# A hybrid diffusion layer on one core: a triangular inversion spread over all four quarters of the matmul array, and narrow products issued as two column halves

## The chip, the core and the metric

The kernel runs on one core of one Trainium2 chip. The metric is the device time of one launch in microseconds, lower is better. A core has a matmul engine (PE in the rows, with its weight loads as PEld), a vector engine (DVE), a scalar engine (ACT), a general engine (POOL), and a queue for transfers (SP). Each runs its own instruction stream in order; they wait for one another through semaphores.

## What is computed

One layer of a hybrid backbone for 512 latent tokens and 128 context tokens. It modulates and projects the tokens, sends them through three mixers (a bidirectional RWKV-7 recurrence, neighbourhood attention, a state-space model), gates and merges them, normalises, and applies a mixture of experts. The part that matters here is the recurrence, per head and per direction:

```python
def step(s, inp):
    r_t, w_t, k_t, v_t, kk_t, b_t = inp
    sa = jnp.einsum('bhvk,bhk->bhv', s, kk_t)
    s = s * w_t[:, :, None, :] - sa[..., None] * b_t[:, :, None, :] + v_t[..., None] * k_t[:, :, None, :]
    return s, jnp.einsum('bhvk,bhk->bhv', s, r_t)
```

The kernel does it in chunks of 128 tokens. Within a chunk the term `sa` makes a 128x128 triangular system per head, and its inverse is built by products of small blocks. The attention is an ordinary softmax over 512 local and 128 context keys per block of 128 queries, then a weighted sum of values of width 64.

## The kernel before

The launch is a row of phases with barriers between them: projections and preparations, the state-space scan, `rwkv_phase`, merge and router, experts, combine. The change lies in `rwkv_phase` alone, in the functions `rwkv_units` and `attention_lane`. Everything is float32; a product (`matmul`) leaves two records on PE in the trace and two weight loads on PEld.

`rwkv_units` walks through ten units (`UNITS`): five chunks of 128 tokens, each in two directions. A unit holds eight heads, as four pairs `q` with two heads `e` each; the head dimension of 64 makes `e` the lower or the upper 64 partitions (`half`). On PE a unit is, in this order:

- five Gram groups `k` = 0 to 4 at L1725, eight products each (64 rows, 128 stationary, 128 moving columns), into the four PSUM banks `bank[0..3]`; k = 0 and 1 are the system matrix and its transpose, and ACT (L1975, L1977), DVE (L1887) and POOL (L2062, L2064) make from them the blocks `lo`, `lc`, `xi`, `yi`;
- two groups of transposes (L1732), four narrow products for a bonus term (L1737, 2 moving columns);
- the inversion of the two 64x64 diagonal blocks in five levels (`LJ - 1`). A level is the group G (L1755, 16 products of 64x64x64 for the eight heads), ACT's copy of it (L1991), then for g = 0 and 1 the groups YG (L1786) and XG (L1791), eight products each; DVE subtracts them from `yi` (L1918) and `xi` (L1920). POOL makes the next level's masked block `lj` (L2071). A product's row half is where its operands lie, its column half is where its output lies; before, both are the same half in all three groups;
- the coupling block of the inverse (L1752 and a last L1786), which uses one quarter of the array;
- the right-hand sides and outputs: L1764 and L1798 (64 rows, 128 stationary, 64 moving), L1767, L1801 and L1819 (128 rows, 128 stationary, 64 moving), eight products each, and the solves and states L1806, L1809, L1814, L1824.

Between these groups PE issues fillers, and each other engine does its share of them at the same points of its own stream. A gate filler ("G", L1349 and L1350) is a piece of a sigmoid gate's product, eight turns for a tile, of which the eighth is empty on PE; ACT applies the sigmoid there. An attention filler ("A") is one of three steps in turn: scores (L1502, L1505), then the weighted sum of the previous block (L1476, L1477, L1479), then the transposes of the probabilities (L1515, L1518). DVE (L1555, L1556, L1558) and ACT (L1597) do the softmax between scores and transposes. Every level has "GA" between G and YG (`FILL_MID`) and "A" after XG (`FILL_LEVEL`). Of 40 attention blocks every fifth is for context queries and has only 128 keys.

## Time and profile before

| | us |
|---|---|
| median of three runs | 2099.69 |
| lowest and highest run | 2098.58, 2108.48 |
| the profiled run, its own time | 2100.16 |
| its span | 2096.8 |
| the ten units, 591.1 to 1219.3 in the span | 628.2 |

The page gives busy times for each engine and the span. The units were located in the timeline of PE by the first Gram products. A timeline row has the start, the duration from the first start to the last end, the engine, line, names, shape and count of records. Matmuls are pipelined, so the last end lies some 0.2 us behind the last issue; the time that a group takes from PE is read from its start to the start of the next group. The granted clock of a stretch is 1.00 at 2.4 GHz and 0.50 at 1.2 GHz.

### The profile page before, as it was taken

What the parts mean: (1) busy time and instruction counts of PE and PEld (TensorE: products, weight loads), DVE (VectorE), ACT (ScalarE), POOL (GpSimd) and SP (SyncE); (2) the same over time, 40 slices, a digit from 0 to 9 for tenths busy, and PEclk for the clock granted to TensorE, in tenths of its full rate; (3) what the DMA queues carried; (4) which work ended last, traced back from release to release, by engine and by line L of the source; (5) the groups of instructions that cost most, each with busy time, mean ns of one, the idle gap of its engine ahead of it and who ended that gap; (6) DMA issues with size and microseconds to landing.
All of it is one profiled execution on the core that took longest, in us unless ns stands there. A gap on an engine that the chain in (4) does not pass through costs nothing. (4 is left out here: it accounts for less than half of the span.)

```text
span 2096.8 us, 40476 instructions
## 1 busy us (share of the span) xinstructions
PE 1914.2 (91%) x15900; PEld 1408.1 (67%) x15900; DVE 1019.3 (49%) x2092; ACT 495.4 (24%) x936; POOL 690.8 (33%) x1036
## 2 busy tenths in 40 slices
PE   7999999888889999999999958998699999999966
PEld 2555655464668877888888738855578888878732
DVE  3868676648345435544555443645622222222238
ACT  2111132130223333433343321101112122112100
POOL 4526000000034323343333223322244454444435
PEclk9999999999899999999999979998799999999988
DMA  9143647473142210222120029610399989999855
GB/s 289 55 136 120 214 160 270 139 271 98 41 139 65 85 48 23 72 69 72 49 74 8 22 95 318 214 43 21 139 358 339 331 303 316 338 339 321 321 227 242
DMA packets 228303, 355.64 MB, mean 170 GB/s; under 512 B 38305, under 2 KB 156852, under 8 KB 224452
## 3 DMA queue, kind: packets, MB, share of 16 engines
q1 hardware_dynamic: 201358, 300.73, 42.2%
q0 software_dynamic: 24496, 45.01, 6.1%
q10 hardware_dynamic: 2310, 7.92, 1.0%
q8 instruction: 102, 1.67, 0.3%
q14 instruction: 37, 0.30, 0.0%
HBM read 307.11 MB, written 84.34 MB: 187 GB/s over the span
## 5 line engine op out<-in xcount | busy, mean ns | idle before, releaser
L2850 DVE TENSOR_TENSOR me_hh<-me_sg,ps_ju 128x128 f32<-128x128 f32 x76 | 21.9, 288 | 386.1 <-PE ps_jd L2802 374.3
L452 PE MATMUL ps_s<-hT,w_in_sb 128*128 128x512 f32 x432 | 194.7, 604 | 0.0
L2794 PE MATMUL ps_jg<-me_xT,me_wg 128*128 128x128 f32 x1216 | 149.3, 276 | 0.0
L1349 PE MATMUL ps_gs<-hT,gt_w 128*128 128x512 f32 x256 | 146.0, 653 | 3.2 <-PEq L76 3.2
L2794 PE MATMUL ps_ju<-me_xT,me_wu 128*128 128x128 f32 x1216 | 148.2, 275 | 0.0
L2802 PE MATMUL ps_jd<-me_wd,me_hh 128*128 128x512 f32 x304 | 143.1, 593 | 2.4 <-DVE me_yb L2856 2.4
L452 PEld LDWEIGHTS ps_s<-hT,w_in_sb 128*128 128x128 f32 x432 | 81.6, 194 | 93.5 <-issue 92.9
L2794 PEld LDWEIGHTS ps_jg<-me_xT,me_wg 128*128 128x128 f32 x1216 | 143.0, 193 | 0.0
L2794 PEld LDWEIGHTS ps_ju<-me_xT,me_wu 128*128 128x128 f32 x1216 | 141.9, 192 | 0.0
L2823 ACT ACTIVATE me_xT<-ps_jx 128x1024 f32<-128x1024 f32 x77 | 78.9, 1025 | 210.4 <-PE ps_jx L2785 210.4
L2785 PEld LDWEIGHTS ps_jx<-ident,me_xg 128*128 128x128 f32 x616 | 79.3, 191 | 69.8 <-DMA me_xg<-h_dram,me_ids 40.6
L2742 POOL TENSOR_TENSOR me_scr<-me_scr 128x1 f32<-128x1 f32 x312 | 61.0, 195 | 185.0 <-DVE me_yb L2856 168.4
L2071 POOL TENSOR_TENSOR rc_lj<-rc_l,rc_lev 128x256 f32<-128x256 f32 x100 | 75.1, 770 | 135.9 <-PE ps_c L1755 135.7
L2785 PE MATMUL ps_jx<-ident,me_xg 128*128 128x128 f32 x616 | 84.7, 281 | 26.6 <-DMA me_xg<-h_dram,me_ids 26.4
L922 DVE SCALAR_TENSOR_TENSOR ad_part<-w_ad_sb,c_silu,ad_part 128x256 f32<-128x256 f32 x224 | 105.2, 511 | 5.8 <-DMA w_ad_sb<-in_w_ada 2.3
L1154 POOL DMA_DIRECT2D out_new_s_re<-s_zz x1 | 0.6, 579 | 312.7 <-DVE s_zz L1218 312.7
L2750 POOL DMA_INDIRECT me_xg<-h_dram,me_ids x80 | 84.3, 1053 | 39.9 <-issue 36.9
L2856 DVE COPY me_yb<-ps_jd 128x1024 f32<-128x1024 f32 x76 | 92.8, 1221 | 4.2 <-issue 4.2
L1350 PEld LDWEIGHTS ps_gp<-hT,gt_w 128*128 128x128 f32 x256 | 50.4, 197 | 64.8 <-issue 64.8
L2761 POOL DMA_INDIRECT yj_dram<-me_yb,me_outs x76 | 77.5, 1020 | 43.4 <-issue 43.4
L2802 PEld LDWEIGHTS ps_jd<-me_wd,me_hh 128*128 128x128 f32 x304 | 52.0, 191 | 39.6 <-issue 36.3
L2030 POOL TENSOR_TENSOR rc_a<-ru_kk,rc_ex 128x512 f32<-128x512 f32 x10 | 12.6, 1265 | 196.8 <-ACT rc_fs L1963 196.8
(569 smaller groups left out, 3985.8 us busy)
## 6 DMA issues: line engine op xcount, KB each, us to landing
me_wg<-in_exp_w_gate SPq DMA_DIRECT2D x76, 512.0 KB, 5.6
me_wu<-in_exp_w_up SPq DMA_DIRECT2D x76, 512.0 KB, 7.7
me_wd<-in_exp_w_down SPq DMA_DIRECT2D x76, 512.0 KB, 6.0
w_ad_sb<-in_w_ada SPq DMA_DIRECT2D x32, 512.0 KB, 4.0
w_in_sb<-in_w_in SPq DMA_DIRECT2D x31, 512.0 KB, 4.4
gt_w<-in_w_in SPq DMA_DIRECT2D x24, 512.0 KB, 4.5
cb_rows<-yj_dram SPq DMA_DIRECT2D x6, 2048.0 KB, 22.0
zr<-in_w_ada SPq DMA_DIRECT2D x4, 2048.0 KB, 8.9
```

The lines of the kernel that those rows point to most:

```text
L452: mm(ps_s[:, b, :], w_in[:, r, k, :], hT[:, k, 0:TS], start=(k == 0), stop=(k == KT - 1))
L922: last = V.scalar_tensor_tensor(o, x, r, o, ALU.mult, ALU.add)
L1349: nc.tensor.matmul(ps_s[:], w[:, t % WR, k, :], hT[:, k, 0:TS], start=(k == 0), stop=(k == KT - 1))
L2071: G.tensor_tensor(lj[:, g], lo[:, g], bc4(levc[:, d, j + 1]), ALU.mult).then_inc(m.c_lj, 1)
L2742: G.tensor_tensor(scr[:, c:c + 1], scr[:, 2:3], scr[:, 2:3], ALU.add)
L2750: G.indirect_dma_start(xg[:, s], None, m.h2_dram, bass.IndirectOffsetOnAxis(ids[:, s:s + 1], axis=0), bounds_check=N - 1, oob_is_err=False ...
L2761: G.indirect_dma_start(m.yj_dram, bass.IndirectOffsetOnAxis(outs[:, b:b + 1], axis=0), yb[:, b], None, bounds_check=N * TOPK - 1, oob_is_e ...
L2785: last = nc.tensor.transpose(ps_x[:, s % 2, k * P:(k + 1) * P], xg[:, s, k:D:KT], m.ident[:])
L2794: last = mm(o[:, 0:P], w[:, s, k, :], xT[:, s % 2, k, :], start=(k == 0), stop=(k == KT - 1))
L2802: last = mm(ps_d[:, ts512(h)], hh[:], wd[:, s, ts512(h)], start=True, stop=True)
L2823: nc.scalar.activation(xT[:, s], ps_x[:, s].rearrange("p (k c) -> p k c", k=KT), ACT.Identity).then_inc(m.j_xt, 1)
L2856: V.tensor_copy(yb[:, b], ps_d[:]).then_inc(m.j_y, 1)
```

## The change

Four things change, all inside the units and the attention filler.

1. G's products write into the other column half than their row half. YG's products go from one row half to the other column half, XG's stay in theirs, and YG and XG are issued in turns, four products for each `q`, so that the four of a turn lie in four different quarters.
2. The Gram groups k = 0 and 1 are cut into 64x64x64 products: 32 for k = 0 (the diagonal blocks twice, once for `lo` in their own partitions and once for `xi` in the other half's) and 24 for k = 1. ACT copies `lo` and `xi` whole and then `lc`, for which it waits for DVE's product on `yi`; DVE makes `yi` in one instruction instead of two; POOL scales `xi` in place.
3. `halves` issues a product with 128 stationary columns as two with 64 each, into the lower and the upper 64 output partitions. It is used for L1737, L1764, L1767, L1798, L1801, L1819 and the attention's weighted sum.
4. DVE subtracts both `yi` first and then both `xi`, where before it went y, x, y, x.

```diff
+def halves(mm, out, l, r, start, stop):
+
+    for b in (slice(0, HD), slice(HD, P)):
+        last = mm(out[b], l[:, b], r, start=start, stop=stop)
+    return last
...
         o = ps_y[:, P:P + HD]
         if i < QT:
             for k in range(4):
-                nc.tensor.matmul(o, pT[:, k * P:(k + 1) * P], zv[:, b, k, hc], start=(k == 0), stop=False)
-            nc.tensor.matmul(o, pT[:, TS:TS + P], cv_sb[:, h, :], start=False, stop=True).then_inc(m.n_pv, 1)
+                halves(nc.tensor.matmul, o, pT[:, k * P:(k + 1) * P], zv[:, b, k, hc], k == 0, False)
+            halves(nc.tensor.matmul, o, pT[:, TS:TS + P], cv_sb[:, h, :], False, True).then_inc(m.n_pv, 1)
         else:
-            nc.tensor.matmul(o, pT[:, TS:TS + P], zv[:, b, QT, hc], start=True, stop=True).then_inc(m.n_pv, 1)
+            halves(nc.tensor.matmul, o, pT[:, TS:TS + P], zv[:, b, QT, hc], True, True).then_inc(m.n_pv, 1)
...
-                    for k, (l, r) in enumerate(((a_, b_), (b_, a_), (k_, a_), (k_, r_), (b_, r_))):
...
+                    rows, cols = coupling(d)
+                    if n:
+                        pe.wait_ge(m.c_un, n)
+                        pe.wait_ge(m.c_s, n)
+                    for q in range(MT):
+                        for e in range(2):
+                            for own, other in ((half[0], half[1]), (half[1], half[0])):
+                                mm(bank[e][own, q, 0:HD], a_[half[e], q, own], b_[half[e], q, own], start=True, stop=True)
+                            for own, other in ((half[0], half[1]), (half[1], half[0])):
+                                last = mm(bank[e][other, q, HD:P], a_[half[e], q, own], b_[half[e], q, own], start=True, stop=True)
+                            if q == MT - 1:
+                                last.then_inc(m.c_gr, 1)
+                    if n:
+                        pe.wait_ge(m.c_y, n * 2)
+                    for q in range(MT):
+                        for e in range(2):
+                            mm(bank[2 + e][rows, q, HD:P], a_[half[e], q, rows], b_[half[e], q, cols], start=True, stop=True)
+                            for own in (cols, rows):
+                                last = mm(bank[2 + e][own, q, 0:HD], b_[half[e], q, own], a_[half[e], q, own], start=True, stop=True)
+                            if q == MT - 1:
+                                last.then_inc(m.c_gr, 1)
...
                             pe.wait_ge(m.c_stage, n + 1)
+                            pe.wait_ge(m.c_L, n * 3 + 2)
+                        if k == 3:
                             pe.wait_ge(m.c_L, n * 3 + 3)
...
-                        last = mm(bank[2][:, 0, 2 * q:2 * q + 2], rkd[:, q, :], m.rkh[:, q, :], start=True, stop=True)
+                        last = halves(mm, bank[2][:, 0, 2 * q:2 * q + 2], rkd[:, q, :], m.rkh[:, q, :], True, True)
...
-                                    last = mm(bank[g][cols, q, 0:HD], lc[rows, g, q, :], yi[rows, g, q, :], start=True, stop=True)
+                                    last = mm(bank[g][rows, q, 0:HD], lc[rows, g, q, :], yi[rows, g, q, :], start=True, stop=True)
                                 else:
-                                    for b in half:
-                                        last = mm(bank[g][b, q, 0:HD], lj[b, g, q, :], yi[b, g, q, :], start=True, stop=True)
+                                    for own, other in ((half[0], half[1]), (half[1], half[0])):
+                                        last = mm(bank[g][other, q, 0:HD], lj[own, g, q, :], yi[own, g, q, :], start=True, stop=True)
...
-                                    mm(bank[2 + e][:, q, 0:HD], a_[half[e], q, :], sts[half[e], q, :], start=(q == 0), stop=False)
+                                    halves(mm, bank[2 + e][:, q, 0:HD], a_[half[e], q, :], sts[half[e], q, :], q == 0, False)
                             for q in range(MT):
                                 for e in range(2):
-                                    last = mm(bank[2 + e][:, q, 0:HD], akt[:, e, q, :], vh(n, 2 * q + e), start=False, stop=(q == MT - 1))
+                                    last = halves(mm, bank[2 + e][:, q, 0:HD], akt[:, e, q, :], vh(n, 2 * q + e), False, q == MT - 1)
...
-                                for b in half if j < LJ - 1 else (cols,):
-                                    last = mm(bank[g][b, q, 0:HD], xi[b, g, q, :], gg[b, g, q, :], start=True, stop=True)
-                            last.then_inc(m.c_yg, 1)
+                                if j == LJ - 1:
+                                    yg = mm(bank[g][cols, q, 0:HD], xi[rows, g, q, :], gg[rows, g, q, :], start=True, stop=True)
+                                else:
+                                    for own, other in ((half[0], half[1]), (half[1], half[0])):
+                                        yg = mm(bank[g][own, q, 0:HD], xi[other, g, q, :], gg[other, g, q, :], start=True, stop=True)
+                                    for b in half:
+                                        xg = mm(bank[2 + g][b, q, 0:HD], gg[b, g, q, :], xi[b, g, q, :], start=True, stop=True)
+                            yg.then_inc(m.c_yg, 1)
                             if j < LJ - 1:
-                                for q in range(MT):
-                                    for b in half:
-                                        last = mm(bank[2 + g][b, q, 0:HD], gg[b, g, q, :], xi[b, g, q, :], start=True, stop=True)
-                                last.then_inc(m.c_xg, 1)
+                                xg.then_inc(m.c_xg, 1)
...
-                            mm(bank[2 + e][:, q, 0:HD], r_[half[e], q, :], sts[half[e], q, :], start=(q == 0), stop=False)
+                            halves(mm, bank[2 + e][:, q, 0:HD], r_[half[e], q, :], sts[half[e], q, :], q == 0, False)
...
-                            mm(bank[2 + e][:, q, 0:HD], rkt[:, e, q, :], vh(n, 2 * q + e), start=False, stop=False)
+                            halves(mm, bank[2 + e][:, q, 0:HD], rkt[:, e, q, :], vh(n, 2 * q + e), False, False)
...
-                            last = mm(bank[2 + e][:, q, 0:HD], rbt[:, e, q, :], un[:, e, q, :], start=False, stop=(q == MT - 1))
+                            last = halves(mm, bank[2 + e][:, q, 0:HD], rbt[:, e, q, :], un[:, e, q, :], False, q == MT - 1)
...
-                    for b in half:
-                        mk = levc[b, 1 - d, 0].unsqueeze(1).unsqueeze(1).to_broadcast([HD, 2, MT, HD])
-                        V.tensor_tensor(yi[b], banks[b, 2:4, :, b], mk, ALU.mult).then_inc(m.c_gd, 1)
+                    mk = levc[:, 1 - d, 0].unsqueeze(1).unsqueeze(1).to_broadcast([P, 2, MT, HD])
+                    V.tensor_tensor(yi[:], banks[:, 2:4, :, 0:HD], mk, ALU.mult).then_inc(m.c_gd, 1)
...
                                 V.tensor_tensor(yi[:, g], yi[:, g], bank[g][:, :, 0:HD], ALU.subtract).then_inc(m.c_yup, 1)
-                                dve.wait_ge(m.c_xg, n * (2 * LJ - 2) + 2 * j + g + 1)
-                                V.tensor_tensor(xi[:, g], xi[:, g], bank[2 + g][:, :, 0:HD], ALU.subtract).then_inc(m.c_xup, 1)
+                        for g in range(2 if j < LJ - 1 else 0):
+                            dve.wait_ge(m.c_xg, n * (2 * LJ - 2) + 2 * j + g + 1)
+                            V.tensor_tensor(xi[:, g], xi[:, g], bank[2 + g][:, :, 0:HD], ALU.subtract).then_inc(m.c_xup, 1)
...
-                    for b in half:
-                        A(lo[b], banks[b, 0:2, :, b], ACT.Identity).then_inc(m.c_L, 1)
+                    A(lo[:], banks[:, 0:2, :, 0:HD], ACT.Identity).then_inc(m.c_L, 1)
+                    A(xi[:], banks[:, 0:2, :, HD:P], ACT.Identity).then_inc(m.c_L, 1)
                     rows, cols = coupling(n % 2)
-                    A(lc[rows], banks[rows, 0:2, :, cols], ACT.Identity).then_inc(m.c_L, 1)
+                    act.wait_ge(m.c_gd, n * 7 + 1)
+                    A(lc[rows], banks[rows, 2:4, :, HD:P], ACT.Identity).then_inc(m.c_L, 1)
...
-                            b = cols if j == LJ - 1 else slice(0, P)
+                            b = rows if j == LJ - 1 else slice(0, P)
...
-                        G.tensor_tensor(xi[:, e], lo[:, e], bc4(levc[:, d, 0]), ALU.mult).then_inc(m.c_xd, 1)
+                        G.tensor_tensor(xi[:, e], xi[:, e], bc4(levc[:, d, 0]), ALU.mult).then_inc(m.c_xd, 1)
```

The issue order of PE in the last level of unit 0, which has no attention filler yet, and up to the first right-hand sides: the rows are the last YG and XG groups, then the coupling block (L1752), the groups on the state and on `akt`, and a gate filler. Before:

```order
L1786 MATMUL ps_c<-rc_g,rc_x 64x64 x8
L1791 MATMUL ps_c<-rc_x,rc_g 64x64 x8
L1752 MATMUL ps_c<-rc_y,rc_lc 64x64 x8
L1764 MATMUL ps_c<-rc_sts,rc_a 128x64 x8
L1767 MATMUL ps_c<-yc,rc_akt 128x64 x8
L1349 MATMUL ps_gs<-hT,gt_w 128x512
L1350 MATMUL ps_gp<-hT,gt_w 128x128
```

After, at the same place (L1813 is YG, L1815 is XG, L1776 the coupling block, L1374 the line of `halves`; the first two rows are one turn of eight that a level has):

```order
L1813 MATMUL ps_c<-rc_g,rc_x 64x64 x2
L1815 MATMUL ps_c<-rc_x,rc_g 64x64 x2
L1776 MATMUL ps_c<-rc_y,rc_lc 64x64 x8
L1374 MATMUL ps_c<-rc_sts,rc_a 64x64 x16
L1374 MATMUL ps_c<-yc,rc_akt 64x64 x16
L1349 MATMUL ps_gs<-hT,gt_w 128x512
L1350 MATMUL ps_gp<-hT,gt_w 128x128
```

YG and XG now alternate two by two, and the two groups behind the coupling block have twice as many products, each half as wide.

The issue order of DVE around the scores of an attention block in a level, before; `rc_y` and `rc_x` are `yi` and `xi`, `at_s` and `at_nmax` the scores and their maximum:

```order
L1852 TENSOR_TENSOR rc_dp<-rc_dm,ru_sig 128x512
L1555 SCALAR_TENSOR_TENSOR at_s<-ps_ax,at_bias 128x512
L1556 TENSOR_SCALAR at_s<-ps_ay 128x128
L1558 TENSOR_REDUCE at_nmax<-at_s 128x1
L1918 TENSOR_TENSOR rc_y<-rc_y,ps_c 128x256
L1920 TENSOR_TENSOR rc_x<-rc_x,ps_c 128x256
L1918 TENSOR_TENSOR rc_y<-rc_y,ps_c 128x256
L1920 TENSOR_TENSOR rc_x<-rc_x,ps_c 128x256
L1564 RECIPROCAL at_rinv<-at_rsum 128x1
```

After:

```order
L1878 TENSOR_TENSOR rc_dp<-rc_dm,ru_sig 128x512
L1562 SCALAR_TENSOR_TENSOR at_s<-ps_ax,at_bias 128x512
L1563 TENSOR_SCALAR at_s<-ps_ay 128x128
L1565 TENSOR_REDUCE at_nmax<-at_s 128x1
L1943 TENSOR_TENSOR rc_y<-rc_y,ps_c 128x256 x2
L1946 TENSOR_TENSOR rc_x<-rc_x,ps_c 128x256 x2
L1571 RECIPROCAL at_rinv<-at_rsum 128x1
```

Both subtractions from `yi` now come before those from `xi`; the softmax work still stands ahead of all four.

## Rows read from the trace of the kernel before

**Rows 1.** The page, first part: busy us, share of the span, instructions

```profile
PE 1914.2 (91%) x15900; PEld 1408.1 (67%) x15900; DVE 1019.3 (49%) x2092; ACT 495.4 (24%) x936; POOL 690.8 (33%) x1036
```

**Rows 2.** Stretches, units 1, 2, sum of ten: us, busy PE, PEld, DVE, ACT, POOL; PEclk

```profile
648.99:709.83 60.84, 60.48 (x874) 50.23 (x873) 32.39 (x71) 23.22 (x51) 23.40 (x25) 1.00 0.19 54
709.83:780.22 70.39, 68.86 (x884) 55.59 (x884) 34.21 (x76) 24.92 (x54) 23.54 (x26) 0.93 0.26 77
...
sum 628.21, PE 615.87 PEld 504.88 DVE 307.60 ACT 223.85 POOL 222.44; mean PE 61.59 PEld 50.49 DVE 30.76 ACT 22.38 POOL 22.24
```

**Rows 3.** Timeline of PE, one level: start, duration in us, engine, line, operation

```profile
722.75 1.15 PE L1755 MATMUL ps_c<-rc_y,rc_lj 64*64 64x64 f32 x32
723.83 1.13 PE L1349 MATMUL ps_gs<-hT,gt_w 128*128 128x512 f32 x2
...
725.65 0.68 PE L1786 MATMUL ps_c<-rc_g,rc_x 64*64 64x64 f32 x16
726.17 0.63 PE L1791 MATMUL ps_c<-rc_x,rc_g 64*64 64x64 f32 x16
726.64 0.63 PE L1786 MATMUL ps_c<-rc_g,rc_x 64*64 64x64 f32 x16
...
727.67 1.12 PE L1502 MATMUL ps_ax<-at_k,at_q 64*128 64x512 f32 x2
```

**Rows 4.** Timeline of PE, the tail of unit 1, Gram groups of unit 2

```profile
692.52 1.11 PE L1764 MATMUL ps_c<-rc_sts,rc_a 64*128 64x64 f32 x16
693.55 2.00 PE L1767 MATMUL ps_c<-yc,rc_akt 128*128 128x64 f32 x16
695.39 1.08 PE L1349 MATMUL ps_gs<-hT,gt_w 128*128 128x512 f32 x2
...
705.59 1.00 PE L1476 MATMUL ps_ay<-at_v,at_pT 128*128 128x64 f32 x8
...
706.65 1.95 PE L1819 MATMUL ps_c<-rc_un,rc_rbt 128*128 128x64 f32 x16
708.53 0.69 PE L1824 MATMUL ps_c<-rc_un,rc_btok 128*64 128x64 f32 x16
...
709.83 1.16 PE L1725 MATMUL ps_c<-rc_b,rc_a 64*128 64x128 f32 x16 [0.36 <-DVE st L1935]
710.80 0.42 PE L1725 MATMUL ps_c<-rc_a,rc_b 64*128 64x128 f32 x4
```

**Rows 5.** Timeline of PE, the end of unit 0's last level

```profile
629.08 0.27 PE L1752 MATMUL ps_c<-rc_y,rc_lc 64*64 64x64 f32 x1
629.12 0.28 PE L1791 MATMUL ps_c<-rc_x,rc_g 64*64 64x64 f32 x3
629.18 0.22 PE L1752 MATMUL ps_c<-rc_y,rc_lc 64*64 64x64 f32 x1
```

**Rows 6.** Timeline of all engines, a level with scores before G

```profile
726.38 0.42 DVE L1918 TENSOR_TENSOR rc_y<-rc_y,ps_c 128x256 f32<-128x256 f32 x1 [0.33 <-PE ps_c L1786]
...
728.94 1.15 PE L1755 MATMUL ps_c<-rc_y,rc_lj 64*64 64x64 f32 x32
729.05 0.69 DVE L1555 SCALAR_TENSOR_TENSOR at_s<-ps_ax,at_bias 128x512 f32<-128x512 f32 x1 [0.84 <-PE ps_ay L1505]
...
729.97 0.82 DVE L1558 TENSOR_REDUCE at_nmax<-at_s 128x1 f32<-128x640 f32 x1
...
730.71 2.98 DVE L1841 TENSOR_TENSOR_SCAN rc_cs<-rc_ones,ru_sig 128x128 f32<-128x128 f32 x4
```

**Rows 7.** Timeline of all engines, the end of a gate tile in unit 2

```profile
754.09 0.66 PE L1515 MATMUL ps_ax<-ident,at_p 128*128 128x128 f32 x4 [1.52 <-ACT at_p L1597]
...
757.79 3.67 PE L1767 MATMUL ps_c<-yc,rc_akt 128*128 128x64 f32 x16
```

**Rows 8.** Timeline of PE, the end of a gate tile in unit 3

```profile
797.86 0.66 PE L1515 MATMUL ps_ax<-ident,at_p 128*128 128x128 f32 x4 [2.42 <-ACT at_p L1597]
```

15 lines of the change are left out of this document (5 added, 10 removed).

## The prediction, made before the changed kernel was run

> **What bounds the kernel now.** I read the page first, for the share of each engine: the matmul engine is busy 91% of the span, the next one 49% [rows 1]. A share over the whole launch says little about one phase, so the second view is the same count by stretches. The change touches the ten units alone, 628.2 us; in them PE is busy 615.9 us, 98%, DVE 307.6, ACT 223.9, POOL 222.4 [rows 2]. So the units are bound by PE's own work, and whatever shortens a group on PE shortens the unit, up to the point where PE arrives before the engine that it waits for. Third, the timeline of PE gives the price of each group, from its start to the start of the next, and the timeline of all engines shows what would come last instead.
>
> **What a record costs.** In a level the eight products of a YG or XG group leave 16 records, which lie in two quarters of the array in turn; 726.17 to 726.64 is 0.47 us, 29 ns a record, so 58.5 ns a record in each quarter [rows 3]. G's 32 records take 1.08 us (722.75 to 723.83), 16 in each quarter: 0.94 us and some 0.14 us of start. With 128 stationary columns 16 records take 1.84 to 1.88 us, 115 ns each [rows 4]. So a load of 64 columns into one quarter or half costs half, and two halves run beside each other. Whether three or four do is the question. Unit 0 has one place that shows it: the single-quarter group L1752 starts at 629.08 while XG still has records to issue, takes its second at 629.18, and XG's three between them start from 629.12 [rows 5]. Three quarters, one of them off the diagonal, ran beside each other with neither pace lost: three records in 58.5 ns, 19.5 ns each. No row shows four, or a long run of three.
>
> **The change, part by part.** All sums are against the profiled execution, 2100.2 us (span 2096.8 and 3.4 around it), 0.5 above the median of the three runs.
>
> (a) YG and XG over four quarters. Before, the four groups of a level take 725.65 to 727.67, 2.02 us [rows 3]. After, the same 64 records lie in four quarters, 16 in each, as G's 32 lie in two: 1.08 us. That is 0.94 us a level, and 50 levels give 47.0 us. Bounds: nothing, if the array takes records no faster than the 29 ns of the two-quarter groups, and 0.94; I take 0.94, since rows 5 show 19.5 ns without strain. G itself only changes its output half: nothing.
>
> (b) L1764 and L1798. 692.52 to 693.55 is 1.03 us [rows 4]. After, 32 records in four quarters, eight in each: 0.47 and 0.15 of start, 0.62. Saves 0.41, twice a unit: 8.2 us, or nothing at 29 ns a record.
>
> (c) L1767, L1801, L1819, with all 128 rows. 1.84, the same, and 1.88 us [rows 4]; after, 16 records in each of two column halves, the 1.08 of G. Saves 2.32 a unit, 23.2 us. This needs two halves only, so it doesn't hang on the four.
>
> (d) L1737: eight records at 115 ns against eight in each half at 58.5, 0.92 against 0.62: 3.0 us.
>
> (e) The attention's weighted sum: ten records, 705.59 to 706.65, 1.06 us [rows 4], or 1.15 by the 115 ns. After, ten in each half, 0.73. I take 0.4 for each of the 32 full blocks and 0.1 for the eight short ones: 13.6 us, bounds 11 and 14.
>
> (f) Gram groups k = 0 and 1. Before, 709.83 to 710.80, 0.97 us for k = 0 [rows 4], and k = 1 alike. After, k = 0 has 64 records and k = 1 has 48. For one head the products go to the quarters of its row half in the order first, second, second, first, so a quarter gets two in a row and PE, which issues in order, waits for it once per head. I count two turns of 117 ns for each `q`: 0.94 and 0.15 for each group. That is 0.1 us a unit more: -1.0 us. At 29 ns a record the two groups would take 3.4 us instead of 2.0, -14 us.
>
> (g) Vector, scalar, general engine. DVE's `yi` product gets shorter, ACT's three copies stay three. ACT's new wait holds `lc` back until DVE's product, and behind it on ACT stand the gate's and the attention's work of the Gram filler; PE has a gate piece, an attention step and k = 2 to issue before k = 3 needs `lc`. I cost it at nothing; uncovered it would be some 0.6 us a unit (estimate: one 64x512 copy).
>
> The sum is 47.0 + 8.2 + 23.2 + 3.0 + 13.6 - 1.0 = 94.0 us of PE work.
>
> **What PE will then wait for.** Four things give part of it back.
>
> First, scores before YG. DVE does the softmax's part before it touches `yi`. PE goes on at 728.94, DVE is at it from 729.05 until 729.97 + 0.82, 1.85 us later [rows 6]; then 0.42 for the first `yi`, and G may start at 2.3. Before, PE had 2.02 and a weighted sum in between, over 3 us. Now it has 1.08 and 0.7, so it waits 0.5 to 0.6 us. Scores stand there in a third of the levels, 12 of them full: 7 us. The new order y, y, x, x helps here, because G's second half needs only the second `yi`.
>
> Second, DVE's scan of the next unit, 2.98 us [rows 6], stands between level 0 and level 1. By the same count it holds up G by 0 to 1 us depending on which attention step is near, on average 0.5 a unit: 5 us.
>
> Third, the ends of gate tiles. ACT then loads its function table twice and PE's eighth turn is empty, so the transposes wait for the softmax: 1.52 us in unit 2 [rows 7], 2.42 in unit 3 [rows 8], and two more of 1.52. ACT's chain doesn't get shorter, so what YG, XG and the weighted sum save in such a level is lost: 1.35 us four times, and 1 us twice where ACT's copy for the attention is late: 7.5 us.
>
> Fourth, unit 0 has no attention filler. Its levels are so short that POOL's `lj` and DVE's scan hold PE by 1.2 and 1.4 us more: 3 us.
>
> To this I add 5 us for the clock. Unit 2 has a stretch at 1.2 GHz behind the wait of 1.52 us: L1767 took 3.46 us there instead of 1.84 [rows 4, 7], the unit 70.4 us where unit 1 took 60.8 [rows 2]. More waits give more occasions, though the longer one in unit 3 [rows 8] was followed by none.
>
> Together 27.5 us are given back, 94.0 - 27.5 = 66.5, and 2100.2 - 66.5 = 2033.7. I say **2034 us**, 3.2% faster. With all of it kept it would be 2006; with twice the waits 2061.
>
> **A rule that speaks against (a).** YG's two products of a turn come from different row halves and write the same PSUM bank, and XG's write a second one. The Trainium skill (TensorEngine Tiling (Array Packing), Restrictions and Gotchas) says that different row tiles cannot access the same bank at the same time. By that, part (a) would bring nothing and the time would be near 2081. The trace disagrees: L1786's products before are in two row halves with one bank, and go at 29 ns a record, twice the pace of one quarter.
>
> **Rivals.** *The issue rate binds.* Four quarters want a record every 14.6 ns; the groups of rows 3 show 29 and rows 5 show 19.5 for a moment. If 29 ns is what PE can take in the long run, (a) and (b) bring nothing and (f) costs 14: 23.2 + 3.0 + 13.6 - 14 = 26 us, of which 2 are given back, since levels stay as long as they are: 2076. For it: every long run of the trace has just this pace. Against: it is exactly twice the pace of one quarter, and rows 5. The Trainium skill (TensorE: Matmul & The Clock Gate, the back-to-back numbers) gives a floor of about 25 ns from start to start however few columns move; by that, an estimate gives (a) some 13 us, (f) -10, and about 2062. The three starts within 58.5 ns in rows 5 are below that floor.
>
> *Slower: the clock.* A unit with a stretch at 1.2 GHz is some 8 us longer than one without, beyond its wait. There are 15 ends of gate tiles; if each brought such a stretch, 13 more than the two there are now (units 2 and 4), that is 104 us: 2034 + 104 = 2138. From nine more on nothing is left of the gain. Against: four of the waits are there already, and only the one in unit 2 was followed by such a stretch within the next microseconds.
>
> *Eaten up.* DVE and ACT, each with its attention work in the way, become the bound in nearly every level, and a level keeps its length: only (b), (c), (d) remain, 34 us, less the waits of the tail, about 20: 2080. Against: DVE is busy 32 of 61 us in a unit, and only a third of the levels has its softmax in the way.
>
> **Chances.** The forecast, 2006 to 2061: 0.70. Issue rate, 2062 to 2079: 0.14. Eaten up, 2075 to 2095, of which 0.02 within 0.5%: 0.07. Slower by the clock: 0.04. Better than 2006, if the waits cost nothing and the stretches at the low clock go: 0.05. A measurement of this kernel can tell about 0.5% from no change, 10 us. Faster 0.93, same 0.03, slower 0.04. The range 2004 to 2076 leaves out less than 2 in 10.
>
> **What would show it.** In the timeline of PE the group of YG and XG should take 1.1 us a level (1.9 to 2.0 under the issue rate), L1374 on `akt` 1.1 (1.84 if halves don't run beside each other), the two Gram groups 2.2 together (3.4). Levels with scores before YG should show a wait of about 0.5 us for DVE's `yi`; PE's share in the units should fall from 98% to 93 to 95%. Wrong would be: a level that keeps its 6.2 us (722.75 to 728.94) [rows 3, 6], or a granted clock clearly under that of rows 2 in most units.

## The result, and the profile after

The changed kernel takes **2032.1 us** in the median of four runs (2021.3 to 2039.7) against 2099.1 us (four runs, 2097.8 to 2108.5): ratio 0.967, 95% interval 0.961 to 0.973. Five more runs, beside eleven of the kernel before, gave 2032.4 and 0.967 (0.965 to 0.969). Forecast were 2034 and a range of 2004 to 2076.

The profiled execution is the fastest of the nine: 2021.3 us. It is compared with rows 1 to 8, which come from one of 2100.2 us.

The page of after, first part, as [rows 1]:

```profile
PE 1820.4 (90%) x17916; PEld 1308.7 (65%) x17916; DVE 1005.0 (50%) x2082; ACT 494.1 (24%) x936; POOL 694.4 (34%) x1036
```

Stretches of after, unit 1 and the sum of the ten, columns as in [rows 2]:

```profile
645.98:697.66 51.68, 50.47 (x1081) 39.87 (x1080) 31.12 (x70) 22.43 (x51) 23.77 (x25) 1.00 0.23 64
...
sum 551.84, PE 520.87 PEld 404.95 DVE 292.97 ACT 221.25 POOL 226.29; mean PE 52.09 PEld 40.50 DVE 29.30 ACT 22.12 POOL 22.63
```

The ten units went from 628.2 to 551.8 us, 76.4 less; the span lost 77.3. So nearly all of it lies where the change was made. PE's busy time there fell from 615.9 [rows 2] to 520.9, by **95.0 us**; what is not busy rose from 12.3 to 31.0, by **18.6 us**. PE is busy 94% of the units, which was 98%.

Timeline of PE, one level of unit 1, as [rows 3]:

```profile
656.90 1.15 PE L1779 MATMUL ps_c<-rc_y,rc_lj 64*64 64x64 f32 x32
...
659.25 0.27 PE L1813 MATMUL ps_c<-rc_g,rc_x 64*64 64x64 f32 x2
...
659.36 0.22 PE L1813 MATMUL ps_c<-rc_g,rc_x 64*64 64x64 f32 x2
659.37 0.23 PE L1815 MATMUL ps_c<-rc_x,rc_g 64*64 64x64 f32 x2
659.42 0.23 PE L1813 MATMUL ps_c<-rc_g,rc_x 64*64 64x64 f32 x2
...
660.34 0.69 PE L1374 MATMUL ps_ay<-at_v,at_pT 128*64 128x64 f32 x16
...
661.57 1.15 PE L1779 MATMUL ps_c<-rc_y,rc_lj 64*64 64x64 f32 x32 [0.43 <-DVE rc_y L1943]
```

YG and XG now stand in one group: 659.25 to 660.34, 1.09 us for the 64 records that took 2.02. Every 58.5 ns (659.36, 659.42) comes a pair of L1813 and a pair of L1815, one record for each quarter: **14.6 ns a record, four quarters at full pace**. What the level then meets is the wait of 0.43 us for DVE's `yi`.

Timeline of PE, tail of unit 1 and both first Gram groups, as [rows 4]; the halves all carry the helper's line L1374:

```profile
645.98 0.36 PE L1723 MATMUL ps_c<-rc_b,rc_a 64*64 64x64 f32 x8
...
646.96 0.22 PE L1732 MATMUL ps_c<-rc_b,rc_a 64*64 64x64 f32 x1
...
648.05 1.13 PE L1349 MATMUL ps_gs<-hT,gt_w 128*128 128x512 f32 x2
...
683.15 1.14 PE L1776 MATMUL ps_c<-rc_y,rc_lc 64*64 64x64 f32 x16
684.08 0.69 PE L1374 MATMUL ps_c<-rc_sts,rc_a 64*64 64x64 f32 x32
684.70 1.15 PE L1374 MATMUL ps_c<-yc,rc_akt 128*64 128x64 f32 x32
685.78 1.12 PE L1349 MATMUL ps_gs<-hT,gt_w 128*128 128x512 f32 x2
...
694.84 0.69 PE L1374 MATMUL ps_ay<-at_v,at_pT 128*64 128x64 f32 x16
...
695.47 1.10 PE L1374 MATMUL ps_c<-rc_un,rc_rbt 128*64 128x64 f32 x32
696.40 0.64 PE L1850 MATMUL ps_c<-rc_un,rc_btok 128*64 128x64 f32 x16
```

What PE waited for in the ten units of after: us in total, times, longest:

```profile
PE ps_ax L1522 <- ACT at_p L1604: 12.4, 4, 3.4
PE ps_c L1779 <- DVE rc_y L1943: 6.2, 11, 0.9
PE ps_c L1779 <- POOL rc_lj L2098: 5.3, 1, 5.3
PE ps_ax L1509 <- ACT at_pT L1612: 1.4, 1, 1.4
PE ps_c L1779 <- issue: 1.3, 1, 1.3
PE ps_c L1723 <- POOL rc_b L2058: 1.0, 1, 1.0
PE ps_c L1750 <- issue: 0.8, 1, 0.8
PE ps_c L1732 <- issue: 0.7, 1, 0.7
PE ps_c L1776 <- DVE rc_y L1943: 0.7, 2, 0.3
```

The same list of the kernel before, which has but one row more:

```profile
PE ps_ax L1515 <- ACT at_p L1597: 7.0, 4, 2.4
PE ps_c L1755 <- POOL rc_lj L2071: 4.4, 1, 4.4
...
PE ps_ax L1502 <- ACT at_pT L1605: 0.3, 1, 0.3
```

The four waits at the ends of gate tiles grew by 5.4 us, a new family of thirteen waits for `yi` costs 6.9, and three new ones, 2.8 us, name no releaser at all (a fourth of 0.3 is further down the list).

**Most of the spread of the runs goes with the granted clock.** After's profiled execution has a span of 2019.5 us and a mean granted clock of 0.956; a second one, of 2042.8 us, has 2041.0 and 0.947 (before: 0.958). (1 - 0.956) x 2019.5 is 88.9 us and (1 - 0.947) x 2041.0 is 108.2: by this estimate 19 of the 21.5 us between two executions of one kernel are time lost at the lower clock. Each run's clock is known, so each time can be given less that loss. That gathers the nine runs of after from 2021 to 2043 into 1928 to 1936, and the table is used below.

It has two limits. It charges the clock for all time at 1.2 GHz, also for time in which PE waits: in the first execution 178.6 us ran at 1.2 GHz and PE was busy in 97.7 of them, in the second 219.2 and 133.5. Half of the busy time, 48.9 and 66.8 us, is what PE can have lost, 17.9 us between the two. So a kernel whose PE waits less in such stretches gains more than the last column says. And the column is not free of noise: the four runs of blocks of two still lie between 1925 and 1946 in it, the five of the tanh gate between 1920 and 1935. Differences of 2 or 3 us in it prove nothing by themselves; where it can be done, the length of single units at a clock of 1.00 is set beside them.

| kernel | runs | median us | mean clock | mean us less the clock's loss |
|---|---|---|---|---|
| before | 11 | 2100.8 | 0.956 | 2008.0 |
| after | 9 | 2032.4 | 0.951 | 1932.7 |
| halves only | 4 | 2054.6 | 0.955 | 1961.4 |
| quarters only | 4 | 2077.1 | 0.950 | 1972.6 |
| y, x, y, x on DVE | 4 | 2031.9 | 0.952 | 1934.7 |
| YG, then XG | 4 | 2043.2 | 0.953 | 1947.4 |
| blocks of two | 4 | 2033.4 | 0.952 | 1934.9 |
| solve in turn | 5 | 2060.4 | 0.947 | 1952.1 |
| solve by lane | 4 | 2037.4 | 0.950 | 1935.5 |
| scores first | 5 | 2035.2 | 0.949 | 1930.5 |
| tanh gate | 5 | 2015.3 | 0.958 | 1929.3 |
| tanh, scores first | 6 | 2012.9 | 0.954 | 1922.1 |
| tanh, scores, solve in turn | 5 | 2041.2 | 0.952 | 1942.7 |

### The profile page after: what moved, and what is told of

Its sections match the earlier page's. It is cut to its first block and busy times, and to the rows that moved or that the text cites. A ratio compares the mean times of both kernels' runs of the same rounds, so it can differ in the third digit from the quotient of the medians.

```text
span 2019.5 us, 44508 instructions
## 1 busy us (share of the span) xinstructions
PE 1820.4 (90%) x17916; PEld 1308.7 (65%) x17916; DVE 1005.0 (50%) x2082; ACT 494.1 (24%) x936; POOL 694.4 (34%) x1036
## 3 DMA queue, kind: packets, MB, share of 16 engines
q8 instruction: 118, 1.93, 0.4%
## 5 line engine op out<-in xcount | busy, mean ns | idle before, releaser
L2829 PEld LDWEIGHTS ps_jd<-me_wd,me_hh 128*128 128x128 f32 x304 | 51.9, 191 | 39.6 <-issue 36.3
L2192 PE MATMUL ps_b<-mg_yh,mg_wh 128*128 128x320 f32 x192 | 61.4, 320 | 16.9 <-DVE mg_yl L2317 10.6
```

The source lines that it names most:

```text
L2192: nc.tensor.matmul(out, w_hi, x_hi, start=first, stop=False)
L2829: last = mm(ps_d[:, ts512(h)], hh[:], wd[:, s, ts512(h)], start=True, stop=True)
```

## The experiments

### Each half of the change alone

Halves only: the kernel before with `halves` at all its places. One of them:

```diff
-                                    mm(bank[2 + e][:, q, 0:HD], a_[half[e], q, :], sts[half[e], q, :], start=(q == 0), stop=False)
+                                    halves(mm, bank[2 + e][:, q, 0:HD], a_[half[e], q, :], sts[half[e], q, :], q == 0, False)
...
```

> The kernel before with the column halves alone (L1737, L1764, L1767, L1798, L1801, L1819 and the attention's weighted sum); inversion and Gram groups as before. Theory (quarters and halves run beside each other, each at 58 ns a record): PE work falls by 8.2 + 23.2 + 3.0 + 13.6 = 48 us, and few waits appear since the levels keep their 2.0 us of YG and XG: 2100 - 48 + 5 = about 2057 us, the groups on akt, rkt and rbt 1.0 us each, those on the state 0.6. Rival (the gain comes from the inversion alone, the halves only double the count of products): 2090 to 2100 and 1.84 us a group.

Quarters only: the changed kernel with the helper made one product again.

```diff
-    for b in (slice(0, HD), slice(HD, P)):
-        last = mm(out[b], l[:, b], r, start=start, stop=stop)
-    return last
+    return mm(out, l, r, start=start, stop=stop)
```

> The changed kernel with halves issuing one full product again, so that only the inversion, the Gram groups and the order on DVE differ from before. Theory: 47 us of YG and XG, 1 us lost in the Gram groups, about 10 us of new waits: about 2064 us. If the parts were independent of each other, the gains of this run and of the one with halves alone would add up to the 67 us of the whole; by my theory they add up to more (some 79), since both shorten what hid the same waits.

Measured: 2054.6 us, ratio 0.977 (0.973 to 0.981), and 2077.1, ratio 0.989 (0.985 to 0.993). The gains, 46 and 24 us, add up to nearly that of the whole, 68, but the second kernel ran at the lower clock. Less the clock's loss they are 46.6 and 35.4 (the second was expected to be 36), 82.0 together, where the whole brings 75.3. The stretch of the ten units shows most of the difference, first halves only, then quarters only (columns as in [rows 2]):

```profile
592.74:1173.79 581.05, 563.82 (x9889) 449.91 (x9888) 307.07 (x676) 223.52 (x486) 223.48 (x242) 0.98 0.21 60
```

```profile
592.21:1190.68 598.47, 577.18 (x9473) 464.21 (x9472) 296.16 (x666) 222.28 (x486) 225.61 (x242) 0.97 0.21 59
```

PE's busy time, 615.9 before, falls by 52.1 and by 38.7, 90.8 together, and by 95.0 with both; the second has a clock of 0.97 where before and after have 0.98, which is a few us of it. So the work adds up. The time that is not busy grows from 12.3 us to 17.2 and to 21.3, by 4.9 and 9.0, and with both by 18.6, or by 15.7 in the second profiled execution of after (556.3 us less 528.2 busy). That is 1.8 to 4.7 more than the sum, where two executions of one kernel differ by 2.9. The single kinds of wait are the same in both executions and say more: the ends of gate tiles grow by 1.7, by 4.8 and with both by 6.5, the sum; the waits for `yi` are none, 2.4 and with both 6.9 us. **Work adds up, the waits for `yi` do not.** Those of 0.43 us stand in neither kernel with one half (quarters only has three longer ones, of 0.80), nor do those without a releaser. The one place where `lc` was late, 0.5 us, is in the kernel with halves only.

### What the order of YG and XG is worth

```diff
-                                    for b in half:
-                                        xg = mm(bank[2 + g][b, q, 0:HD], gg[b, g, q, :], xi[b, g, q, :], start=True, stop=True)
...
+                                for q in range(MT):
+                                    for b in half:
+                                        xg = mm(bank[2 + g][b, q, 0:HD], gg[b, g, q, :], xi[b, g, q, :], start=True, stop=True)
```

> The changed kernel with YG's eight products of a g issued before XG's eight, in the same four quarters as now, not in turns of four. Theory (PE issues in order and holds at the first product whose quarter is busy, so only neighbours in the order run beside each other): the group of YG and XG goes back from 1.1 to about 1.9 us a level, and the time to about 2070 us. Rival (each quarter has a queue deep enough to look past the other group): 1.1 us stays and so does the time, 2032.

Measured: 2043.2 us, ratio 0.972 (0.968 to 0.976), between the two expectations. That of strict issue fell. Timeline of PE, the same group:

```profile
660.04 0.51 PE L1813 MATMUL ps_c<-rc_g,rc_x 64*64 64x64 f32 x10
660.34 0.27 PE L1818 MATMUL ps_c<-rc_x,rc_g 64*64 64x64 f32 x2
660.38 0.28 PE L1813 MATMUL ps_c<-rc_g,rc_x 64*64 64x64 f32 x3
...
661.54 0.45 PE L1374 MATMUL ps_ay<-at_v,at_pT 128*64 128x64 f32 x8
```

The group takes 1.50 us, neither 1.1 nor 1.9. XG's first record starts when ten of YG's sixteen have started; the last six, three in each of two quarters, follow beside it. So PE had issued past products that still waited for their quarter. The 0.41 us more in each of 50 levels are 20.5; some 7 come back, since the waits for `yi` fall from 6.9 to 1.5 us and those at the ends of gate tiles from 13.8 to 11.7, and less the clock's loss the kernel is 14.7 behind after. If three records a quarter is the depth, blocks of two products a quarter are nearly as good as turns by one:

```diff
+                                for pair in ((0, 1), (2, 3)):
+                                    for q in pair:
+                                        for own, other in ((half[0], half[1]), (half[1], half[0])):
+                                            yg = mm(...)
+                                    for q in pair:
+                                        for b in half:
+                                            xg = mm(...)
```

> The changed kernel with YG and XG issued in blocks of two column blocks (four products YG, four products XG, twice a lane half) where it issues them in turn by one. With all of YG ahead of XG the group took 1.50 us for 1.09, and XG's first record started when ten of YG's sixteen had, so three records a quarter were waiting in place. If that is the depth to which issued products wait at a busy quarter, blocks of four records a quarter cost little: 1.09 to 1.15 us a level, 2032 to 2035. If instead issue stops at the first product whose quarter is busy, half of each block runs on two quarters: about 1.5 us a level and 2043 to 2050.

Measured: 2033.4 us, ratio 0.969 (0.966 to 0.973), and 1.14 us a group (663.43 to 664.57), 0.05 more than in turns by one. That is the first of the two expectations.

The order y, y, x, x on DVE, put back to y, x, y, x:

```diff
-                        for g in range(2 if j < LJ - 1 else 0):
-                            dve.wait_ge(m.c_xg, n * (2 * LJ - 2) + 2 * j + g + 1)
-                            V.tensor_tensor(xi[:, g], xi[:, g], bank[2 + g][:, :, 0:HD], ALU.subtract).then_inc(m.c_xup, 1)
+                                dve.wait_ge(m.c_xg, n * (2 * LJ - 2) + 2 * j + g + 1)
+                                V.tensor_tensor(xi[:, g], xi[:, g], bank[2 + g][:, :, 0:HD], ALU.subtract).then_inc(m.c_xup, 1)
```

> The changed kernel with DVE's order y, x, y, x in a level as before. Theory: in the levels with scores before YG, G's second half waits some 0.35 to 0.45 us more for the second yi, elsewhere nothing: 3 to 5 us more, 2036, hardly to be told from the spread of the runs but to be seen in the trace as split G groups. Rival (the order carries the gain, since DVE decides every level): 20 us or more.

Measured: 2031.9 us, ratio 0.966 (0.961 to 0.971), with the same waits of 0.43 us. By the times the new order on DVE is worth nothing that these runs can tell. The trace shows what was expected in kind, smaller: G behind a wait starts as before, but its second half comes later, and 13 of the 50 G groups take 1.27 us (661.44 to the gate filler at 662.72) instead of 1.08. That is 0.19 each, 2.5 us in all, where 3 to 5 were expected:

```profile
661.44 1.34 PE L1779 MATMUL ps_c<-rc_y,rc_lj 64*64 64x64 f32 x32 [0.43 <-DVE rc_y L1943]
```

### More of the same: the solve in turn

The solve's two kinds of product, one lane half each, issued in turn so that both halves have work.

```diff
-                    for e in range(2):
-                        for q in range(MT):
                             last = mm(u_ps[rows, e, q, :], yx[:, e, q, :], rhs[:, e, q, :], start=True, stop=True)
```

> The changed kernel, with the products of the solve step (those between the waits on y and the products of L1842) issued with their two lane halves taken in turn rather than one half's four and then the other's four, so that two row halves of the array have work at one time. By the theory that what the change bought is parts of the array that run beside each other (a product of one quarter beside three others is 14.6 ns a record, a product alone in its half 58), the two groups of eight products fall by near a half, some 0.9 us in a unit and 9 us in ten: 2023. By the rival, that the waits of ACT and DVE on the first half of the results set this place (the first half's four products now end as late as the second's), the saving is taken back: 2032 or up to 3 more.

Measured: 2060.4 us, ratio 0.981 (0.978 to 0.983): 28 us **slower** than after. Both expectations were wrong. Timeline of PE:

```profile
699.51 0.33 PE L1832 MATMUL ps_c<-rc_rhs,rc_y 64*64 64x64 f32 x2
699.76 0.33 PE L1833 MATMUL ps_c<-rc_rhs,rc_yx 128*64 128x64 f32 x2
700.02 0.32 PE L1832 MATMUL ps_c<-rc_rhs,rc_y 64*64 64x64 f32 x2
```

The two kinds don't only differ in the lane half: one has 64 rows, the other 128. A pair of products takes 0.51 us where it took 0.23. Between the last record of one and the first of the next lie 0.148 us instead of 0.058, and the next but one comes after 0.107: **0.14 us for each change between 64 and 128 rows**. From first to last record the solve takes 3.95 us for 2.00; 14 more changes at 0.14 are 1.96. Ten units make 19.5 us, and that is what the table gives (1952.1 to 1932.7); by its estimate the other 8 us are clock. Blocks of four put it to the test:

```diff
                         for q in range(MT):
                             mm(u_ps[cols, e, q, :], yi[cols, e, q, :], rhs[cols, e, q, :], start=True, stop=True)
-                    for e in range(2):
                         for q in range(MT):
                             last = mm(u_ps[rows, e, q, :], yx[:, e, q, :], rhs[:, e, q, :], start=True, stop=True)
```

> The changed kernel with the solve's two kinds of product alternated in blocks of four and not of one: L1832's have 64 active rows, L1835's 128. Alternated one by one they took 3.96 us for 2.00, and the step from the last record of one kind to the first of the other was 0.148 us where two records of one kind stand 0.058 apart, with 0.107 to the next. If each change between 64 and 128 rows costs (0.148 - 0.058) + (0.107 - 0.058) = 0.14 us, three changes where there was one make the group 2.28 us: 2.8 us in ten units, 2035. If the loss came from the turn between the two lane halves in PSUM and not from the row count, blocks of four give no more than one further step: 2.0 to 2.1 us.

```profile
691.52 0.67 PE L1832 MATMUL ps_c<-rc_rhs,rc_y 64*64 64x64 f32 x8
692.13 0.68 PE L1834 MATMUL ps_c<-rc_rhs,rc_yx 128*64 128x64 f32 x8
```

One block takes 0.61 us with its change, 692.13 less 691.52. From first to last record the solve takes 2.28 us for 2.00, two more changes at 0.14, as expected. Measured 2037.4 us; less the clock's loss 2.8 more than after, which is within the noise of that column, but unit 1, at a clock of 1.00 in both, lasts 51.96 us instead of 51.68, 0.28 more.

Neither run separates the row count from the other thing that changes with it, the column half that the product writes. Groups of one row count do: the two parts of each L1374 product on `akt` write the two column halves in turn, and 32 records take 1.08 us, and YG's and XG's products change column half within every turn at 14.6 ns a record. Changing the column half alone costs nothing.

### The waits that the change brought

Scores ahead of YG, on the levels that carry them:

```diff
-                            fill(FILL_MID)
+                            fill("AG" if n and (2 * n + 2 * j) % 3 == 2 else FILL_MID)
```

> The changed kernel, with PE's step of the score products put ahead of the products YG on the levels that carry scores (the waits of 0.43 us ahead of the y products L1779 stand on the levels behind which no other work of PE lies). Theory A, a level ends at DVE: those waits are time of PE that nothing fills, and work put ahead of YG does not fill them; what it does is to take the 0.4 to 0.9 us that ACT and DVE need before YG's operands are there. Seven waits of 0.43, one of 0.46, two of 0.34, two of 0.90 and one of 0.94 us stand in the units, 6.9 us together; if the scores lie in the place of the waits the median falls from 2032 by up to 7, to 2025. Theory B, the wait only moves: the chain lj, Gamma, y, x of one level is as long as before and the scores now lie on it, so that the level gets longer by what it saved: 2032, or up to 7 us more. The trace tells them apart: under A the rows of L1779 show no wait over 0.2 us on those levels, under B a like wait stands ahead of L1813.

Measured: 2035.2 us, ratio 0.969 (0.967 to 0.971), no gain against after, where theory A had up to 7 us. Most of the waits did go:

```profile
PE ps_c L1779 <- DVE rc_y L1943: 1.8, 3, 0.9
```

In after it was 6.2 us in eleven places. Units 1, 5 and 7, without a wait on issue, lasted 51.2, 51.4 and 50.5 us instead of 51.7, 51.9 and 51.0, so the wait did not move either, and theory B falls. But the median shows none of it. The mean clock is 0.949, and waits without a releaser are 5.2 us in the profiled run, where the two executions of after have 3.1 and 3.9; whether the edit brings either is not shown.

The gate by tanh, three instructions of ACT in place of two, and no change of function table between the gate and the softmax:

```diff
-            nc.scalar.activation(gs[:, t % 2, 0:TS], ps_s[:], ACT.Sigmoid)
-            nc.scalar.activation(gs[:, t % 2, TS:N], ps_p[:, 0:TP], ACT.Sigmoid).then_inc(m.b_sg, 1)
+            nc.scalar.activation(gs[:, t % 2, 0:TS], ps_s[:], ACT.Tanh, scale=0.5)
+            nc.scalar.activation(gs[:, t % 2, TS:N], ps_p[:, 0:TP], ACT.Tanh, scale=0.5).then_inc(m.b_th, 1)
+            act.wait_ge(m.b_th, t - GT_S5 + 1)
+            nc.scalar.activation(gs[:, t % 2], gs[:, t % 2], ACT.Copy, scale=0.5, bias=0.5).then_inc(m.b_sg, 1)
```

> The changed kernel, with the gate worked out on ACT as 0.5 tanh(x/2) + 0.5 in three instructions instead of the sigmoid in two: the function table of ACT then needs no reload between the gate's function and the exponentials. It is for the four waits of PE of 2.97, 3.44, 2.97 and 2.97 us at the ends of the gate's tiles, which were 1.52, 2.42, 1.52 and 1.52 before the change. Theory A: what PE waits for there is ACT, with its table loads (1.28 us each) on the path; without them two loads a place go and one more instruction comes, and the waits fall to 1 or less: 4 x 2 to 2.5 = 8 to 10 us, and up to 3.4 us more where the low clock that follows three of these waits stays away (half of each stretch of 3.4 to 6.8 us is lost): 2020, 2017 to 2024. Theory B: the wait is for DVE or the queue of an output, and the table loads lie beside it: 2032, waits of about 3 us in the same four places.

Measured: **2015.3 us**, ratio 0.958 (0.956 to 0.961), clear of after's interval and a little below the 2017 to 2024 of theory A. ACT at the end of a gate tile in unit 2, after:

```profile
733.97 1.28 ACT L1362 ACT_TABLE_LOAD   x1
735.26 0.60 ACT L1362 ACTIVATE gt_s<-ps_gs 128x512 f32<-128x512 f32 x1
735.76 0.27 ACT L1363 ACTIVATE gt_s<-ps_gp 128x128 f32<-128x128 f32 x1
736.05 1.28 ACT L1604 ACT_TABLE_LOAD   x1
737.34 0.83 ACT L1604 ACTIVATE at_p<-at_s,at_nmax 128x640 f32<-128x640 f32 x1
```

and with tanh:

```profile
733.72 0.59 ACT L1362 ACTIVATE gt_s<-ps_gs 128x512 f32<-128x512 f32 x1
734.20 0.28 ACT L1363 ACTIVATE gt_s<-ps_gp 128x128 f32<-128x128 f32 x1
734.51 0.74 ACT L1365 ACTIVATE gt_s<-gt_s 128x640 f32<-128x640 f32 x1
735.16 0.81 ACT L1606 ACTIVATE at_p<-at_s,at_nmax 128x640 f32<-128x640 f32 x1
```

PE waits for the softmax that ends this chain: 0.90 us instead of 2.97 (twice 1.28 less, an instruction more), 4.1 instead of 12.4 in four places. What PE waited for was ACT with its loads, as in theory A. The Trainium skill (ScalarE: Activation LUTs, What ACT_TABLE_LOAD costs) adds a drain of about 1.38 us to each load's 1.28. Here the first load ends as the next instruction starts, 1.29 us after its own start, and the second starts 0.02 us after the instruction ahead of it ends (735.76 and 0.27): no row has room for the drain, and the measurement decides for 1.28.

The waits are only part of the gain. Twelve microseconds around the first of these waits, in after's second profiled execution (clock is the column behind POOL's):

```profile
738.00:750.00 12.00, 9.03 (x161) 7.51 (x158) 2.39 (x8) 7.57 (x16) 0.30 (x1) 0.72 0.01 1
```

and with tanh:

```profile
733.00:745.00 12.00, 11.10 (x273) 9.07 (x270) 4.84 (x13) 6.28 (x17) 4.01 (x4) 1.00 0.01 3
```

A granted clock of 0.72 over 12 us is 6.7 us at 1.2 GHz. The four places of that run show 0.72, 0.72, 0.86 and 0.86, those of after's first profiled execution 1.00 and three times 0.86, and with tanh they show 1.00 each, the level of 2.4 GHz. The four units that hold them (2, 3, 8 and 9) took 228.8 us in the first execution and 232.7 in the second, with tanh 215.2: 13.6 and 17.5 less. 8.3 of that are the waits; the other 5.3 and 9.2 are near what the granted clock of the four places makes, (1 - clock) x 12 each, 5.0 and 10.1 us. So of the 17 us by the medians about half is wait and about half is clock. The table has 3.4 for the part without the clock, which is too little: here PE stands still in a part of the slow stretches (busy 9.03 of the 12 us above), and the column charges the clock for it.

Tanh and scores first together:

> The changed kernel with the gate by tanh (2015 alone, where it shortened the four waits at the ends of the gate's tiles from 2.97 and 3.44 to 0.90 and 1.37 us) and the scores ahead of YG on the levels that carry them (alone no gain in the median, though the three units that nothing else touches each lost 0.5 to 0.6 us). If the gain of the second was real and hidden by more time at the low clock (51 us of it inside the stage against 31), the two together give 2015 - 10 x 0.5 = 2010. If the chain of the level took it back, 2015.

Measured: 2012.9 us, ratio 0.958 (0.956 to 0.960), the lowest median here, but not apart from tanh alone, and between the two expectations of 2010 and 2015. The trace tells more. Units 1 to 9 have a clock of 1.00 in both profiled executions, first tanh alone, then with the scores first:

```profile
645.84:1128.35 482.51, 468.81 (x9709) 365.23 (x9708) 273.97 (x621) 180.34 (x439) 204.49 (x216) 1.00 0.22 62
```

```profile
649.04:1127.38 478.34, 468.39 (x9709) 364.95 (x9708) 275.29 (x621) 181.76 (x439) 203.50 (x216) 1.00 0.22 62
```

4.2 us are gained there, 3.8 of them time in which PE was not busy, near the 4.8 us by which the waits for `yi` fell. So the gain of the scores is real where no slow stretch lies. Of it the medians show 2.4; that the clock outside the stage took the rest, 0.954 for 0.958 in the mean, is not shown.

All three edits:

> The changed kernel with the three edits of the other runs together: scores ahead of YG on the levels that carry them, the solve's products in turn, the gate by tanh. If each takes away a wait or work of PE on the path, they add: 7 + 9 + 12 = 28 us, 2004. If they take from the same slack of the engines around PE (DVE above all, which is not faster by any of them), the sum is well short of it: 2015 or more.

Measured: 2041.2 us, ratio 0.971 (0.969 to 0.973). The number lies in the second expectation, 2015 or more, but not for its reason: the solve's edit is a loss and not a gain. Less the clock's loss it is 20.6 us above the kernel with tanh and scores first, the 14 changes of row count in ten units once more.

And the changed kernel itself once more:

> The changed kernel itself once more, beside the three others of this call: its four runs so far lie between 2021 and 2040. If what spreads them is the stretches of TensorE's low clock outside the changed stage (178.6 us of low clock in its profiled execution, 201 to 209 in those of four kernels that differ from it in the changed stage alone), the five new runs fall in 2020 to 2040 with the lower granted clock on the longer times: 0.956 stands beside 2021 and 0.949 beside 2037 and 2040. If the gain of an edit is to be read at all it must stand above that spread.

Measured: 2032.4 us (2027.9 to 2042.8), one of the five above the expected 2020 to 2040. The lowest clock, 0.947, stands beside the longest time and the highest, 0.954, beside the shortest.

## Why the prediction was right, step by step

**The work.** Forecast 94.0 us, measured 95.0 in PE's busy time. (a) 1.09 for 1.08 us: 0.93 x 50 = 46 for 47.0. (b) `rc_sts` by `rc_a` 684.08 to 684.70, 0.62 as forecast. (c) 1.08 and 1.08, but for `rc_rbt` 0.93 in three units (695.47 to 696.40 in unit 1) and 0.98 in seven, where 1.08 was forecast: 24.2 for 23.2. (d) 0.56 for 0.88, 0.32 us a unit for 0.30. (e) 0.63 for the 1.06 of [rows 4], 0.43 for 0.4. (f) 0.98 and 1.09 us, 2.07 for 2.18. Here two slips met: the forecast's own figures, 2.18 against twice 0.97, make 0.24 us a unit and not the 0.1 that it wrote, and the pair had taken 1.99 before (709.83 to 711.82). The measured loss, 0.08 us, fits the 1.0 in ten units by luck. (g) no wait on `lc`, as costed.

The pace of 19.5 ns on which (a) rested was right, but the rows shown for it don't hold it: L1752's second record comes 0.10 us after its first [rows 5]. Its third and fourth, at 629.24 and 629.30, come 0.06 apart with XG's two a step beside them; that is the pace, for a step or two.

Two things were missed in it, small and of one cause. Where a group meets one of another tile shape, up to 0.14 us is paid: 0.09 between the two (0.148 less 0.058) and 0.05 behind the second's first record (0.107 less 0.058). The products of L1374 have the shape 64*64 where L1776 stands ahead, and 128*64 behind the weighted sum. The rows of before: L1752 took 1.07 us with a group 64*128 behind it,

```profile
691.45 1.14 PE L1752 MATMUL ps_c<-rc_y,rc_lc 64*64 64x64 f32 x16
```

to the 692.52 of [rows 4]; after, 683.15 to 684.08, it takes 0.93 to the next. The same 0.14 is missing at `rc_rbt` in unit 1, whose neighbours on both sides have its shape; where the one ahead has another, the group takes 0.98. I had taken it for a start cost of each group; these rows and the runs on the solve show that it hangs on a change of shape. Not every change costs it: between L1819 and L1824, from 128 columns to 64 with all rows, the first group takes 1.83 to 1.93 us, and its 16 records at 115 ns are 1.84.

**Issue rate** (chance 0.14): fell at once, 14.6 ns a record over 64 records. With it fall, for this kernel, the floor of 25 ns that the Trainium skill gives (TensorE: Matmul & The Clock Gate, the back-to-back numbers) and its rule on one PSUM bank and two row tiles, by which part (a) would have brought nothing (TensorEngine Tiling (Array Packing), Restrictions and Gotchas): L1813's two products of a turn are just that case and lose nothing.

**What was given back.** Scores and scan, forecast 7 + 5: the waits for `yi` are 6.9 us. Their place was right, 0.43 for the 0.5 to 0.6 forecast. The separate 5 us for the scan were counted on top and hardly came: it stands ahead of two of the thirteen waits, 0.46 us at 721.16, and 0.94 at 946.38 where the scores stand too. Gate-tile ends, forecast 7.5: 12.4 + 1.4 - 7.0 - 0.3 = 6.5, +1.45 three times and +1.02 once for the 1.35 forecast. Unit 0, forecast 3: 5.3 - 4.4 + 1.0 = 1.9. Not forecast: 3.1 us on issue and 0.6 for a transpose in the last unit (L1536). The list makes 19.0, PE's busy time 18.6, for 22.5; in the second profiled execution it is 15.7, mostly since unit 0's wait for `lj` is 2.1 us there and 5.3 here.

**The clock** was costed at 5 us, and by the table's estimate it is 7: the mean loss is 92.9 us in the eleven runs of before and 100.0 in the nine of after. In the profiled execution it was nothing (0.958 and 0.956), which is one reason why that one is 11 us under the median. So 95.0 of work, less 18.6 of waits, less 7 of clock, is 69.4 us; the medians differ by 67.0 in the first runs and 68.4 in all. Forecast were 66.5. The mechanism held in every term, but the nearness is partly luck: 4 us too much in waits, the scan's 5 above all, against 1 too little in work and 2 too little in clock.

**Eaten up** fell: levels got shorter by what their products did, less 0.43 where the softmax is in the way. **Slower by the clock** fell in size, not in kind: the clock has a price, by that estimate a tenth of the gain.

## What to carry to other kernels

Price a chain of small products by the quarter (here 58.5 ns a record in each, with four beside each other), not by the engine; order them so that no quarter gets more than two products before the others get theirs (here 0.05 us a group of 64 records, and 0.41 with four in a row), and keep products of one row count together (0.14 us a change). When the engine that sets the end gets faster, look through the trace for the places where it already waits a little: those waits grow by all that was saved ahead of them, here by 1.45 us, and the clock may charge for them again. Before two kernels that are 1% apart are compared, read single runs with their granted clock beside them, and then stretches that ran at one clock in both: they settled what the medians could not.

## What the runs showed of the hardware that I had not expected

- A change between products of 64 and of 128 rows costs 0.14 us (0.148 and 0.107 between starts, for 0.058): 14 more in a unit took 1.95 us, two more 0.28.
- Issue does not stop at a busy quarter: XG's records began while three issued records of YG were still waiting in each of two quarters.
- Two executions of one kernel differ by 21.5 us, of which 18 to 19 are granted clock by either estimate. A kernel with fewer waits of PE does not always have a higher one: scores first took away 4.8 us of waits for `yi` and ran at 0.949 for 0.951, which the spread of the runs does not tell apart; taking 2.07 us from each of the long waits gave 0.958. What decides stays open.
- Waits of PE that no engine releases (0.2 to 3.6 us each, two to five in the units) stand in kernels with both halves of the change and in neither that has one. PE has 17916 records for 15900 in the whole launch. That its instructions come too late there is a guess; no run tested it.
